# Paired head values, a shorter router chain and output rows scaled at the copy out, in a two-layer decoder step on one core

## The chip, the cores and the metric

The kernel runs on one core of one Trainium2 chip. It is one launch, written in Bass, in which each engine has its own program and waits on semaphores by hand: TensorE (PE), VectorE (DVE), ScalarE (ACT), GpSimd (POOL), and SyncE (SP), which issues most of the DMAs. The metric is the device time of one execution in microseconds; the figure for a kernel is the median of its runs.

## The reference

One inference step of a two-layer decoder for 512 prompt tokens and 8 sample tokens (520 in all), model width 1024, float32.

```python
# layer 0: stick-breaking attention (8 heads of 64) beside a causal pooling; layer 1: a convolution module
z = einsum(q, k) * d ** -0.5 + bias_h
log_stay = where(causal, log_sigmoid(-z), 0)
between = cumsum(log_stay, reverse over keys) - log_stay
weight = where(causal, exp(log_sigmoid(z) + between), 0);  o = weight @ v
# both layers: hierarchical mixture of experts on x = rmsnorm(h)
g_logits = x @ w_rg + b_rg            # 4 groups, the best one
e_logits = x @ w_re + b_re            # 4 experts in it, the best two
y = sum over the two: combine * (silu(x @ w_gate[e]) * (x @ w_up[e])) @ w_down[e]
h = h + y;  h = h + sigmoid(rmsnorm(h) @ w_pg + b_pg) * (p @ w_ple)
# at the end
y = rmsnorm(h, norm_final)
```

## The kernel before

The residual stream stands transposed in SBUF as `hT`: 8 tiles of 128 channels by 520 tokens. Dense products go through four PSUM slots of two banks in one fixed order of jobs (`dense_plan`); `fill_wait` lets TensorE fill a slot when the job four before it has been drained by ScalarE or VectorE, and `drain_wait` waits for the fill.

**Attention (from L1798).** The scores of a head against the keys of four key blocks are 512 + 384 + 256 + 128 = 1,280 columns, the causal part. One pass per head h goes: TensorE makes the scores of head h + 1 (L1810) and the values of head h - 1 (L1838); ScalarE copies the logits out (L930), VectorE takes -|z| (L1314), ScalarE the exponential and the logarithm (L932, L933), VectorE makes log(1 + exp z) (L1318), GpSimd zeroes the upper triangle of the four diagonal blocks (L713), TensorE sums these over later keys with ten products, a triangle of ones on the diagonal block and full ones for each later block (L1827), VectorE subtracts the sums (L1327), ScalarE takes the exponential (L923), and GpSimd masks again. The logits of three heads are held at once (`zs3`). On GpSimd the mask of the weights of head h - 1 stands ahead of the mask for the sticks of head h. Between these TensorE multiplies the cached values of one of eight sample tokens per head (L1854, eight products in four groups of output partitions) and turns the result (L1861); VectorE copies it (L1338).

The ten products of a head, and the values of one head, each in the output partitions of its parity:

```python
for kb in range(4):
    for src in range(kb, 4):
        ins = mm(..., tri[:] if src == kb else ones[:], sp[:, at[src]:at[src] + width], ...)
...
for kb in range(4):
    ins = mm(ps[rows, 6, kb * P:TP], v_tok[:, kb, h * DH:(h + 1) * DH], zs3[h % 3][...], ...)
```

**Router (L1383 to L1468 on VectorE, L1897 to L1943 on TensorE).** After each layer's last output projection, the squares of `hT` are summed over channels by two products with ones that put the sum on all partitions (L1716); ScalarE takes the root (L893); five products turn it to one column per block of 104 tokens (L1917), beside the turned logits (L1914); VectorE takes the reciprocal and the rest of the choice in operations of 5 to 100 columns. TensorE counts the ranks of the tokens with fifteen products (L1931), VectorE makes twenty comparisons against running numbers (L1445, L1446), TensorE multiplies them into a table of token rows (L1939), and VectorE turns the table into indices (L1459 to L1466). In the meantime ScalarE scales the turned token rows (L965) and stores them, 104 at a time, to DRAM (L968), from where GpSimd gathers the rows of each expert with an indirect DMA (L761). GpSimd waits for the whole table, the stores and a cleared buffer before the first gather.

**Experts.** Weights stream through a ring of six buffers; ScalarE and VectorE split them and the tokens into a high and a low part (L986, L1478 and L990, L1482), TensorE multiplies the parts (L1957 to L1959), and the result rows are scattered (L766). The first expert's tokens go: gather, eight transposes (L1699), ScalarE's part (L990), VectorE's part (L1482). VectorE has the low parts of four weight halves (L1478) ahead of L1482.

**End.** The last gated update of `hT` and the squares overlap. Then come the sum over channels (L1716), the root (L893), a reciprocal on 128 x 520 (L1204), eight products with the gain (L1207), eight transposes per block of 128 tokens (L1699), a copy by ScalarE into one of two buffers (L876), and a store that GpSimd issues (L847, L849).

## Time and profile before

| | us |
|---|---|
| median of 3 runs | 1520.71 (1519.55 to 1520.96) |
| the profiled execution, its own time | 1512.51 |
| its span in the trace | 1510.8 |
| TensorE busy (matmul) | 1337.0, 88% of the span |
| VectorE, ScalarE, GpSimd busy | 1022.6, 702.9, 239.7 |
[...]

The profile is one execution on the chip. Times are from the start of the span; L numbers are lines of the kernel. A line of the timeline gives the start, the length, the engine, the operation, its operands and how many were merged; in brackets, how long the engine had been idle and what released it. A float32 product counts as two instructions. The chain that ended last is followed back from the last instruction, at each step to what released it.

### The profile page before, as it was taken

The numbers are of one execution on the slowest core, as the hardware profiler recorded it, in microseconds if no ns is written. First come the engines' busy times: TensorE is split into PE (matmuls) and PEld (weight loads), VectorE is DVE, ScalarE is ACT, GpSimd is POOL, SyncE is SP. The second block draws the span as 40 slices with busy tenths as digits, with TensorE's granted clock in tenths as the row PEclk, the third lists the DMA queues.
The fourth block names the chain that finished last, engine by engine and source line by source line (L and its number), as shares of the span: only waits on it lengthen the run. The fifth ranks groups of instructions, "written<-read, shape, count | busy, mean of one in ns | idle before, by whom it ended". The sixth has DMA issues, their size and how long they took to land. (4 is left out here: it accounts for less than half of the span.)

```text
span 1510.8 us, 16104 instructions
## 1 busy us (share of the span) xinstructions
PE 1337.0 (88%) x6141; PEld 1044.2 (69%) x6142; DVE 1022.6 (68%) x1071; ACT 702.9 (47%) x685; POOL 239.7 (16%) x224
## 2 busy tenths in 40 slices
PE   2899899896699999998979999899489999998893
PEld 2686355585488878886768884578478878887772
DVE  3268944315798878885754999523598878885854
ACT  1010244114477768773620007223467767785532
POOL 1033321200213323210000000100112322211000
PEclk7899899997699999999989999999599999999996
DMA  6448436207489999986460302013279999994201
GB/s 258 181 175 350 152 133 251 59 1 279 135 320 374 303 374 376 373 334 238 138 223 0 112 16 100 3 34 109 71 270 386 386 303 388 389 371 180 111 0 57
DMA packets 122740, 314.05 MB, mean 208 GB/s; under 512 B 10060, under 2 KB 10720, under 8 KB 120608
## 3 DMA queue, kind: packets, MB, share of 16 engines
q1 hardware_dynamic: 106350, 249.82, 45.8%
q0 software_dynamic: 14256, 58.69, 10.8%
q10 hardware_dynamic: 2074, 4.71, 0.9%
q8 instruction: 42, 0.69, 0.2%
q14 instruction: 18, 0.15, 0.0%
HBM read 304.17 MB, written 26.70 MB: 219 GB/s over the span
## 5 line engine op out<-in xcount | busy, mean ns | idle before, releaser
L1727 PE MATMUL ps<-xnT,ring 128*128 128x260 f32 x1408 | 315.8, 388 | 13.0 <-DVE xnT L1207 7.1
L1727 PEld LDWEIGHTS ps<-xnT,ring 128*128 128x128 f32 x1408 | 271.9, 193 | 56.4 <-issue 14.4
L1958 PE MATMUL ps<-ring_parts,arena_parts 128*128 128x512 f32 x768 | 308.3, 401 | 0.0
L1478 DVE TENSOR_TENSOR ring_parts<-ring,xnT_parts 128x2048 fp32r<-128x2048 f32 x96 | 219.3, 2292 | 45.1 <-ACT xnT_parts L986 44.0
L1478 DVE TENSOR_TENSOR ring_parts<-ring,arena_parts 128x2048 fp32r<-128x2048 f32 x96 | 219.4, 2291 | 40.7 <-ACT arena_parts L986 40.4
L986 ACT ACTIVATE xnT_parts<-ring 128x2048 fp32r<-128x2048 f32 x96 | 183.5, 1917 | 85.3 <-PE ps L1959 76.7
L986 ACT ACTIVATE arena_parts<-ring 128x2048 fp32r<-128x2048 f32 x96 | 183.4, 1918 | 71.7 <-PE ps L1959 48.5
L1958 PEld LDWEIGHTS ps<-ring_parts,arena_parts 128*128 128x128 f32 x768 | 148.5, 193 | 31.1
L1957 PE MATMUL ps<-xnT_parts,arena_parts 128*128 128x512 f32 x384 | 159.1, 414 | 10.1 <-DVE arena_parts L1482 10.1
L1957 PE MATMUL ps<-arena_parts 128*128 128x512 f32 x384 | 155.5, 405 | 8.9 <-DVE arena_parts L1482 5.2
L1959 PE MATMUL ps<-xnT_parts,arena_parts 128*128 128x512 f32 x384 | 155.6, 405 | 0.0
L1959 PE MATMUL ps<-arena_parts 128*128 128x512 f32 x384 | 151.5, 395 | 0.0
L766 POOL DMA_INDIRECT y_rows<-arena,tab_i x32 | 61.7, 1928 | 470.3 <-ACT arena L998 470.3
L1699 PE MATMUL ps<-ident,arena 128*128 128x128 f32 (+5 forms) x617 | 89.7, 293 | 50.5 <-DMA arena<-x_rows,tab_i 17.7
L1699 PEld LDWEIGHTS ps<-ident,arena 128*128 128x128 f32 (+5 forms) x617 | 78.5, 151 | 63.9 <-issue 22.7
L1649 DVE SCALAR_TENSOR_TENSOR arena<-arena,wdw 128x512 f32<-128x512 f32 x150 | 112.8, 752 | 6.0 <-DVE arena L1669 0.3
L761 POOL DMA_INDIRECT arena<-x_rows,tab_i x32 | 81.7, 2553 | 177.7 <-DVEq L1468 166.3
L1957 PEld LDWEIGHTS ps<-xnT_parts,arena_parts 128*128 128x128 f32 x384 | 75.0, 195 | 28.2 <-DVE arena_parts L1482 11.4
L885 ACT ACTIVATE sq<-hT 128x520 f32<-128x520 f32 x56 | 35.1, 634 | 125.9 <-DVE hT L1365 91.6
L1957 PEld LDWEIGHTS ps<-arena_parts 128*128 128x128 f32 x384 | 73.4, 191 | 25.3 <-issue 5.6
L876 ACT ACTIVATE arena<-ps 128x520 f32<-128x520 f32 (+4 forms) x29 | 21.8, 758 | 143.8 <-PE ps L1727 84.5
L1959 PEld LDWEIGHTS ps<-xnT_parts,arena_parts 128*128 128x128 f32 x384 | 74.7, 194 | 18.2
(283 smaller groups left out, 1704.7 us busy)
## 6 DMA issues: line engine op xcount, KB each, us to landing
ring<-in_w_gate_e SPq DMA_DIRECT2D x32, 2048.0 KB, 16.5
ring<-in_w_up_e SPq DMA_DIRECT2D x32, 2048.0 KB, 16.8
ring<-in_w_down_e SPq DMA_DIRECT2D x32, 2048.0 KB, 17.6
ring<-in_w_in_ab SPq DMA_DIRECT2D x4, 2048.0 KB, 26.7
ring<-in_w_ple_gate SPq DMA_DIRECT2D x4, 2048.0 KB, 8.1
ring<-y_rows SPq DMA_DIRECT2D x16, 512.0 KB, 6.6
ring<-in_w_in_c SPq DMA_DIRECT2D x4, 2048.0 KB, 8.7
x_rows<-arena ACTq DMA_DIRECT2D x10, 416.0 KB
```

The source lines that it names most:

```text
L761: pool.indirect_dma_start(xg[:, e % GATHERS, :], None, x_rows[layer], bass.IndirectOffsetOnAxis(ap=tab_i[:, 0, e * BLK:e * BLK + 1], axis= ...
L766: pool.indirect_dma_start(y_rows[layer], bass.IndirectOffsetOnAxis(ap=tab_i[:, 1, e * BLK:e * BLK + 1], axis=0), yo[:, e % 2, :], None, bo ...
L876: nc.scalar.activation(dst, src_of(s), ACT.Copy).then_inc(s_drained["act"], 1)
L885: nc.scalar.activation(sq[:, k % 2, 0:T], src[:, k, :], ACT.Square).then_inc(s_sq, 1)
L986: nc.scalar.activation(high[hu0 % 4], unit(n)[:, at:at + HU], ACT.Copy).then_inc(s_hi, 1)
L1478: v.tensor_tensor(w_lo, w, high[hu0 % 4].bitcast(F32), ALU.subtract).then_inc(s_lo, 1)
L1649: link(v.scalar_tensor_tensor(y, x, tap, y, ALU.mult, ALU.add))
L1699: return nc.tensor.transpose(dst, src, ident[0:n, 0:n])
L1727: ins = mm(s[:, half, 0:HALF], w[:, k, :], src[:, k, half * HALF:(half + 1) * HALF], start=(k == 0), stop=(k == n - 1))
L1957: mm(ps[:, bank, :], x, w, start=start, stop=False)
L1958: mm(ps[:, bank, :], x, w_lo, start=False, stop=False)
L1959: return mm(ps[:, bank, :], x_lo, w, start=False, stop=stop)
```

## The change

It does five things. In attention, GpSimd masks the sticks of a head before the weights of the head ahead of it, and adds up the masked blocks of later keys itself, in `spare`, so that TensorE needs one triangle and one ones product per key block, seven in place of ten. The values of two heads are multiplied together, block by block in turn, once both heads' weights are masked; for that the logits stand in four buffers, the fourth over queries and keys that are used up (`qk` holds both, tile by tile), and the turned sample results follow one head later. In the router the squares are summed per token by five products with one column of ones, the ranks come from five products over several blocks at once, the twenty comparisons become three wide operations, and the row indices are written four steps earlier, with a semaphore of their own, while the first scatter waits for the whole table. At the end ScalarE multiplies `hT` by the gain while the squares are made, the transposes start from that, token sums give the root, and the last copy scales each row by its reciprocal; there are five output buffers, and SP issues the stores.

```diff
+LOGIT_BUF = (0, 1, 2, 0, 1, 3, 2, 0)
+LOGIT_FREE = (0, 0, 0, 2, 2, 0, 4, 4)
...
-        qT = ar(4, T)
-        kT = ar(4, T)
+        qk = ar(4, 2, T)
+        qT, kT = qk[:, :, 0, :], qk[:, :, 1, :]
...
-        zs3 = [zs[:, 0, :], zs[:, 1, :], xnT[:, 4:KT, :].rearrange("p k t -> p (k t)")[:, 0:1280]]
+        zs3 = [zs[:, 0, :], zs[:, 1, :], xnT[:, 4:KT, :].rearrange("p k t -> p (k t)")[:, 0:1280],
+               arena[:, 0:1280]]
+        spare = [xnT[:].rearrange("p k t -> p (k t)")[:, 3360:4000], sq[:].rearrange("p a b -> p (a b)")[:, 0:640]]
...
-        ar = Arena()
-        y_tok = ar(2, D)
+        y_tok = shaped(arena[:, 3112:3112 + 5 * D], (5, D))
...
 # SyncE, at its end (and taken out of GpSimd's program)
+            for i in range(5):
+                sp.wait_ge(s_drained["act"], JOBS[("y", i)][2])
+                ...
+            sp.wait_ge(s_yt, 16 * 5)
...
 # GpSimd
             for h in range(SBH):
+                pool.wait_ge(s_sp, h + 1)
+                sp, later = ex[:, h % 2, :], spare[h % 2]
+                link(mask(sp))
+                pool.tensor_copy(later[:, 0:P], sp[:, 1024:1024 + P])
+                pool.tensor_copy(later[:, 256:256 + P], sp[:, 512:512 + P])
+                link(pool.tensor_tensor(later[:, P:256], sp[:, 1024 + P:1280], sp[:, 896:1024], ALU.add))
+                pool.tensor_tensor(later[:, 256 + P:640], sp[:, 512 + P:896], later[:, 0:256], ALU.add
+                                   ).then_inc(s_spm, 1)
                 if h:
                     mask_weights(h - 1)
-                pool.wait_ge(s_sp, h + 1)
-                mask(ex[:, h % 2, :]).then_inc(s_spm, 1)
...
-                pool.wait_ge(s_tab, routed + 1)
+                pool.wait_ge(s_rows_of, layer + 1)
...
+                    if not e:
+                        pool.wait_ge(s_tab, routed + 1)
                     pool.wait_ge(s_y, NE * layer + e + 1)
...
 # ScalarE
-                if h >= 3:
-                    act.wait_ge(s_pv, h - 2)
+                if LOGIT_FREE[h]:
+                    act.wait_ge(s_pv, LOGIT_FREE[h])
...
+            def final_rows(k):
+                nc.scalar.activation(xnT[:, k, :], hT[:, k, :], ACT.Copy, scale=prm[:, G_FIN + k:G_FIN + k + 1]
+                                     ).then_inc(s_hg, 1)
...
-                norm(i, upd, squared=KT)
+                s = drain_wait(act, "norm", i)
+                nc.scalar.activation(rs[:, 22, 0:NRT], s[0:RT, 0, 0:NRT], ACT.Sqrt, bias=eps[0:RT, :], scale=MULT
+                                     ).then_inc(s_drained["act"], 1)
...
                         square(3 if layer == 0 else 7, m - 2, hT)
+                        if layer:
+                            final_rows(m - 2)
...
-            norm(6, "ple1", squared=KT - 2)
+            for k in range(KT - 2, KT):
+                h_wait(act, "ple1", k)
+                square(7, k, hT)
+                final_rows(k)
+            s = drain_wait(act, "norm", 6)
+            nc.scalar.activation(rms[:, 0:4], s[:, 0, 0:4], ACT.Sqrt, bias=eps[:], scale=MULT)
+            ...
+            act.wait_ge(s_ytok, 1)
             for i in range(5):
-                if i >= 2:
-                    act.wait_ge(s_yt[i % 2], 16 * (i // 2))
                 n = P if i < 4 else TS
-                copy_out("y", i, y_tok[0:n, i % 2, :].rearrange("p (a b) -> p a b", a=2), lambda s: s[0:n, :, :])
+                s = drain_wait(act, "y", i)
+                nc.scalar.activation(y_tok[0:n, i, :].rearrange("p (a b) -> p a b", a=2), s[0:n, :, :], ACT.Copy,
+                                     scale=rstd[0:n, i:i + 1]).then_inc(s_drained["act"], 1)
...
 # VectorE
+                dve.wait_ge(s_drained["act"], JOBS[("norm", 1 if layer == 0 else 4)][2])
+                link(v.reciprocal(rs[:, 21, 0:NRT], rs[:, 22, 0:NRT]))
+                dve.sem_inc(s_rtok, 1)
                 s = drain_wait(dve, "turned", layer)
...
-                for n in range(10):
-                    v.tensor_scalar(sel_c[:, n, :], iot, ten(15)[:, n:n + 1], None, ALU.is_equal)
-                    ins = v.tensor_scalar(sel_b[:, n, :], iot[:, 0:NE * BLK], ten(16)[:, n:n + 1],
-                                          vl[:, n:n + 1], ALU.is_equal, ALU.mult)
-                ins.then_inc(s_sel, 1)
+                link(v.tensor_tensor(sel_b, steps_of(NE * BLK), wide(ten(16), NE * BLK), ALU.is_equal))
+                v.tensor_tensor(sel_c, steps_of(CAP), wide(ten(15), CAP), ALU.is_equal)
+                v.tensor_tensor(sel_b, sel_b, wide(vl, NE * BLK), ALU.mult).then_inc(s_sel, 1)
...
-                link(v.tensor_tensor(tabf[:, 0, :], tabf[:, 1, :], tabf[:, 2, :], ALU.add))
+                v.tensor_tensor(tab_i[:, 0, :], tabf[:, 1, :], tabf[:, 2, :], ALU.add).then_inc(s_rows_of, 1)
+                v.tensor_tensor(tabf[:, 0, :], tabf[:, 1, :], tabf[:, 2, :], ALU.add)
...
-            norm(6, "ple1", G_FIN, added=KT - 3)
+            for k in range(KT - 3, KT):
+                add_square(7, k)
+            dve.wait_ge(s_drained["act"], JOBS[("norm", 6)][2])
+            v.reciprocal(rstd[:, 0:4], rms[:, 0:4])
+            ...
...
 # TensorE
+            def token_sums(i, rows, count):
+                s = fill_wait(pe, "norm", i)
+                pe.wait_ge(s_sqadd, 8 * (sq_seen[0] + 1))
+                for n in range(count):
+                    last = min(T, (n + 1) * rows)
+                    ins = mm(s[0:last - n * rows, 0, n:n + 1], rstd[:, n * rows:last], ones[:, 0:1], start=True, stop=True)
+                filled(ins)
+                sq_seen[0] += 1
...
                 for kb in range(4):
+                    col, width = c0 + at[kb], TP - kb * P
+                    ins = mm(ps_flat[:, col:col + width], tri[:], sp[:, at[kb]:at[kb] + width],
+                             start=True, stop=(kb == 3), skip_group_check=True)
+                    if kb < 3:
+                        ins = mm(ps_flat[:, col + P:col + width], ones[:], behind[kb], ...)
...
-            def values(h):
+            def values(p):
+                pe.wait_ge(s_wm, 2 * p + 2)
+                if p:
+                    pe.wait_ge(s_ot, p)
                 for kb in range(4):
+                    for h in (2 * p, 2 * p + 1):
+                        rows = slice(64 * (h % 2), 64 * (h % 2) + 64)
+                        ins = mm(ps[rows, 6, kb * P:TP], v_tok[:, kb, h * DH:(h + 1) * DH], ...)
+                ins.then_inc(s_pv, 2)
...
             for h in range(SBH):
                 if h + 1 < SBH:
                     scores(h + 1)
-                if h:
-                    values(h - 1)
+                if h >= 2:
+                    sample_values(h - 2)
+                    if h % 2 == 0:
+                        values(h // 2 - 1)
                 sticks(h)
...
+            sample_values(SBH - 2)
+            pe.wait_ge(s_dd, SBH)
+            turn_sample(SBH - 3)
             sample_values(SBH - 1)
-            values(SBH - 1)
-            pe.wait_ge(s_dd, SBH)
             turn_sample(SBH - 2)
+            values(SBH // 2 - 1)
             turn_sample(SBH - 1)
...
+                for far in range(NRT):
+                    ins = mm(s[0:RT, 0, far * NE:NRT * NE], ones[0:RT, 0:RT] if far else before[0:RT, 0:RT],
+                             flat_cnt[:, 0:(NRT - far) * NE], start=(far == 0), stop=(far == NRT - 1), ...)
...
-            square_sums("norm", 6)
             for i in range(5):
                 s = fill_wait(pe, "y", i)
                 rows = P if i < 4 else TS
                 for k in range(KT):
-                    xn_wait(k)
+                    if not i:
+                        pe.wait_ge(s_hg, 2 * KT + k + 1)
+                    if not i and k == KT - 1:
+                        token_sums(6, P, 5)
                     ins = tr(s[0:rows, k // 4, (k % 4) * P:(k % 4 + 1) * P], xnT[:, k, i * P:i * P + rows], P)
```

## Rows read from the trace of the kernel before

**Rows 1.** Busy time by stage: stretch, length, each engine's busy time, PEclk, DMA share, GB/s.

```profile
1085.00:1390.00 305.00, 295.47 (x1333) 240.96 (x1334) 253.13 (x164) 219.75 (x155) 67.05 (x34) 0.97 0.92 332
```

**Rows 2.** Timeline of TensorE in attention, one head: start, length, line, operation.

```profile
216.85 1.90 PE L1854 MATMUL ps<-ring,arena 128*8 128x512 f32 x16
...
221.03 2.37 PE L1838 MATMUL ps<-xnT,arena 128*64 128x512 f32 x8
...
224.24 1.11 PE L1827 MATMUL ps<-arena,tri 128*128 128x512 f32 x2
...
228.75 1.90 PE L1854 MATMUL ps<-ring,arena 128*8 128x512 f32 x16
```

**Rows 3.** Timelines of ScalarE, VectorE and GpSimd around the same head.

```profile
225.33 1.36 ACT L933 ACTIVATE arena<-arena,one 128x1280 f32<-128x1280 f32 x1
...
230.39 1.27 ACT L923 ACTIVATE arena<-arena 128x1280 f32<-128x1280 f32 x1 [3.70 <-DVE arena L1327]
...
228.86 1.49 DVE L1327 TENSOR_TENSOR arena<-arena,ps 128x1280 f32<-128x1280 f32 x1 [0.65 <-PE ps L1827]
...
230.73 0.69 DVE L1338 COPY arena<-ps 128x512 f32<-128x512 f32 x1 [0.37 <-PE ps L1854]
...
231.73 2.00 POOL L713 TENSOR_SCALAR_AFFINE_SELECT arena<-arena 128x128 f32<-128x128 f32 x8 [8.76 <-ACT arena L923]
...
291.83 2.66 POOL L758 MEMSET arena<- 128x3072 f32 x1
```

**Rows 4.** The chain that ended last, layer 1's router: start, length, what.

```profile
1047.46 1.09 PE ps L1917 x10
...
1048.98 0.27 DVE arena L1390
...
1056.41 2.91 PE ps L1931 x30
...
1063.06 0.29 DVE arena L1445
...
1067.57 4.53 PE ps L1939 x20
...
1072.33 0.25 DVE arena L1459
...
1074.94 5.79 DMA arena<-x_rows,tab_i
...
1080.98 1.96 PE ps L1699 x8
...
1084.01 1.24 DVE arena_parts L1482
```

**Rows 5.** Layer 0's router: timeline, and DMA rate from 365 to 385 in 40 slices.

```profile
371.00 0.31 ACTq L968 DMA_DIRECT2D x_rows<-arena  x1
...
378.50 3.06 POOL L761 DMA_INDIRECT arena<-x_rows,tab_i  x1 [84.01 <-DVEq L1468]
...
GB/s 418 401 434 430 410 414 401 406 434 406 389 360 311 328 324 340 336 332 332 356 344 344 160 45 0 0 0 0 0 0 0 0 0 0 66 66 123 180 91 41
```

**Rows 6.** The chain that ended last, at the end.

```profile
1480.27 2.09 PE ps L1716 x4
...
1501.07 1.02 ACT arena L876
```

**Rows 7.** Timeline of TensorE, the convolution's fold.

```profile
939.52 1.94 PE L2186 MATMUL ps<-xnT,ident 128*64 128x512 f32 x8 [0.30 <-PE ps L2174]
```

**Rows 8.** Timeline of TensorE, second head's sticks and seventh head's values.

```profile
200.41 1.13 PE L1827 MATMUL ps<-arena,tri 128*128 128x512 f32 x2
...
268.52 2.37 PE L1838 MATMUL ps<-arena 128*64 128x512 f32 x8 [2.14 <-POOL arena L713]
```

**Rows 9.** Busy time in short stretches at the start of attention; PEclk stands third from last.

```profile
176.00:180.00 4.00, 3.36 (x5) 1.72 (x6) 4.00 (x2) 0.58 (x1) 0.00 (x0) 0.50 0.98 301
...
188.00:192.00 4.00, 4.00 (x9) 2.42 (x8) 1.97 (x2) 1.93 (x2) 0.00 (x0) 0.50 0.94 332
```

More of the change, by code:

```diff
@@ L377, in decoder_step @@
         s_rc = sem("s_rc")
+        s_rows_of = sem("s_rows_of")
         s_wrg, s_rtok, s_hg = sem("s_wrg"), sem("s_rtok"), sem("s_hg")
@@ L404, in decoder_step @@
         s_acc, s_xc, s_lnx, s_silu = sem("s_acc"), sem("s_xc"), sem("s_lnx"), sem("s_silu")
-        s_yt = [sem(f"s_yt{i}") for i in range(2)]
+        s_yt, s_ytok = sem("s_yt"), sem("s_ytok")
         s_cvf = sem("s_cvf")
@@ L1324, in attend_back @@
             def attend_back(h):
-                zb = zs3[h % 3]
+                zb = zs3[LOGIT_BUF[h]]
                 dve.wait_ge(s_cf, h + 1)
@@ L1818, in sticks @@
                     pe.wait_ge(s_dd, h)
-                if h >= 2:
-                    turn_sample(h - 2)
+                if h >= 3:
+                    turn_sample(h - 3)
                 pe.wait_ge(s_spm, h + 1)
-                sp = ex[:, h % 2, :]
+                sp, later = ex[:, h % 2, :], spare[h % 2]
+                behind = (later[:, 256:640], later[:, 0:256], sp[:, 896:1024])
                 for kb in range(4):
-                    for src in range(kb, 4):
-                        off = (src - kb) * P
-                        width = TP - src * P
-                        ins = mm(ps_flat[:, c0 + at[kb] + off:c0 + at[kb] + off + width],
-                                 tri[:] if src == kb else ones[:], sp[:, at[src]:at[src] + width],
-                                 start=(src == kb), stop=(src == 3), skip_group_check=True)
@@ L1908, in _ @@
                 filled(ins)
-                square_sums("norm", 1 if layer == 0 else 4)
+                token_sums(1 if layer == 0 else 4, RT, NRT)
                 s = fill_wait(pe, "turned", layer)
@@ L1913, in _ @@
                 for i in range(NRT):
-                    mm(s[0:RT, 0, i * 21:i * 21 + 20], lparts[:, i * RT:(i + 1) * RT], fold[:], start=True, stop=True)
-                pe.wait_ge(s_drained["act"], JOBS[("norm", 1 if layer == 0 else 4)][2])
-                for i in range(NRT):
-                    ins = mm(s[0:RT, 0, i * 21 + 20:i * 21 + 21], rms[:, i * RT:(i + 1) * RT], ident[:, 0:1],
-                             start=True, stop=True)
+                    ins = mm(s[0:RT, 0, i * 20:i * 20 + 20], lparts[:, i * RT:(i + 1) * RT], fold[:], start=True, stop=True)
                 filled(ins)
@@ L1928, in _ @@
                 pe.wait_ge(s_cnt, layer + 1)
-                for i in range(NRT):
-                    for src in range(i + 1):
-                        ins = mm(s[0:RT, 0, i * NE:(i + 1) * NE],
-                                 before[0:RT, 0:RT] if src == i else ones[0:RT, 0:RT], cnt[:, src, :],
-                                 start=(src == 0), stop=(src == i))
+                flat_cnt = cnt.rearrange("p i e -> p (i e)")
+                for far in range(NRT):
+                    ins = mm(s[0:RT, 0, far * NE:NRT * NE], ones[0:RT, 0:RT] if far else before[0:RT, 0:RT],
+                             flat_cnt[:, 0:(NRT - far) * NE], start=(far == 0), stop=(far == NRT - 1),
+                             skip_group_check=True)
                 filled(ins)
```

47 lines of the change are left out of this document (20 added, 27 removed).

## The prediction

> **What bounds the kernel now.** I read the stage table of busy time first. It shows two expert stages of about 305 us each, in which TensorE is busy nearly throughout [rows 1] and nothing of the change is at work, and three other places that the diff touches: the attention heads (172 to 286 us), the two routers (347 to 389 and 1043 to 1085 us) and the end (from 1473 us). For these I read each engine's timeline and the chain that ended last.
>
> *Attention.* TensorE is the bound: a head takes 228.75 - 216.85 = 11.90 us without a gap: sample values and next scores 4.18, the values of one head and one turned sample 3.21, sticks 4.51 [rows 2]. ScalarE, VectorE and GpSimd finish in its shadow [rows 3].
>
> *Routers.* One engine waits for the next, mostly in small operations; the chain of layer 1 is in [rows 4]. In layer 0 another thing is late too: the last row store is issued at 371.00, the DMA engines fall silent after 376.5, and the first gather starts at 378.50 [rows 5].
>
> *End.* After the last squared tile comes a serial chain: a sum over all channels from 1480.27, a root, a reciprocal of 128 x 520, eight products, transposes, and copies that take turns in two buffers; the last starts at 1501.07 in a span of 1510.8 [rows 6].
>
> **The change, part by part.**
>
> *Sticks.* The ten products of a head stream 2,560 columns; with the sums made beforehand there are seven, of 2,048. 4.51 x 0.8 = 3.61: 0.9 us a head off TensorE [rows 2].
>
> *Paired values.* Two heads write to the two halves of the output partitions in turn. The fold of the convolution does the same now: four products of 512 columns, in halves, take 1.94 [rows 7], 0.95 ns a column. One head's values, 1,280 columns alone, take 2.37 [rows 2], 1.85 ns a column. So halves run side by side, and a pair costs 2.3 in place of 4.6.
>
> TensorE's own work for two heads is then 2 x 4.18 + 3.21 + 0.9 + 2 x 3.61 = 19.7 against 23.8. That is not what decides. The pair's values wait for the weights of its second head, and these come out of a long loop: values and turn 3.21, sticks 3.61, next scores and sample values 4.18, two VectorE copies of 0.69, VectorE's first pass 1.49, exponential 1.27, logarithm 1.36, second pass 1.49, subtraction 1.49, exponential of the weights 1.27, four masks 1.0 [rows 2, 3]. (The three passes are all over 1,280 columns and so are both exponentials; one row of each stands.) That is 21.8, with some nine handovers of 0.05 about 22.2 a pair. TensorE idles some 2.5 us a pair ahead of the values, and a pair gains 1.6, not 4.1. Three such rounds, the first still filling: 4.5.
>
> At the start there is more. Now the second head's sticks begin at 200.41 [rows 8], behind the first values. Afterwards no values stand there, and the stick mask no longer queues behind the weights' mask: they can start when the scores end, around 197. That is 3.5.
>
> GpSimd gets, per head, two copies of 128 columns and sums of 128 and 384: 768 columns of operations that the trace of before does not show. Eight masks of 128 columns take 2.00 [rows 3], which gives 1.5 us; the memset at 2.66 per 3,072 columns gives 0.7, the low end; twice the mask, 3.0, since a sum reads two operands, is the high one. I take 1.5, the row nearest in kind. It is then hidden: subtraction and weights take 2.8, and GpSimd masks and sums for 2.5. Attention: **-8 us** (ends -3.5 and -9.5).
>
> *Row sums.* With a sum per token, five turning products fall away (from 1047.46) and the root shortens. The product with the logits at 1048.98 can start at 1047.3: -1.7 [rows 4].
>
> *Rank.* Thirty instructions, 2.91, become ten, about 1.1: -1.8 [rows 4].
>
> *Comparisons.* Twenty small ones, from 1063.06 to just ahead of 1067.57, become three of 800, 1,280 and 800 columns. From 0.27 at 100 columns and 1.49 at 1,280 a column costs 1.03 ns: 1.0 + 1.5 + 1.0 = 3.5 in place of 4.4: -0.9 [rows 3, 4].
>
> *Table.* The gathers may go after four steps of 0.25 in place of eight, 1.1 earlier. But the first tokens end at VectorE at 1084.01, and VectorE splits four weight halves between the last step and then; these are done only 0.7 ahead of 1084.01. So -0.7 [rows 4]. GpSimd's added wait for the whole table stands ahead of the first scatter, an expert later: it costs nothing.
>
> Layer 1: 1.7 + 1.8 + 0.9 + 0.7 = **-5 us**. Layer 0 has the same steps, but its row stores share the DMA engines with weights. The last store, issued at 371.0, is landed at 376.5 at the latest; it can go out about 1.3 us earlier, so a gather waits until 375 or so in place of 378.5: **-3 us** (ends -2 and -5) [rows 5].
>
> *End.* ScalarE applies the gain while squares are made, so the transposes need only unscaled rows, and the root enters in the last copy. The last square is some 0.4 later for the copies ahead of it: sums may start at 1480.7. Five of them at half clock, at 4.53 / 10 each as in the table product: 2.3. Two roots and two reciprocals of a few columns, with handovers: 0.9. The first copy starts at 1483.9. The other transposes follow the sums, 1.96 a tile at half clock [rows 4]: tiles at 1485.3, 1487.3, 1489.2, the sample rows at 1490.2. Their copy, 1.0, ends at 1491.2 in place of 1502.1, and what comes after, a store and the close, is taken as it was: **-11 us** (ends -9 and, with the full clock back early, -14). Five buffers cost nothing; SP, which takes the stores over, has nothing else left to issue.
>
> The sum: -8 - 3 - 5 - 11 = -27. The profiled execution took 1512.51, so it would be 1485.5; the runs shown have a median of 1520.71, 0.5% above it, and I carry that over: **1494 us**.
>
> **Rivals.**
>
> *Short spells at half clock in attention.* [...] The new waits are 2 to 4 us. If three of them are each followed by 4 us at half clock, attention gains 3.5 in place of 8: 1498 to 1500. Chance 0.15.
>
> *GpSimd is slow.* At 3.0 us of new work a head, its sums end after the weights, and the second head's mask stands behind them: 1.4 to 2 us a pair longer, attention -3, total 1499. The trace shows only masks there, mostly beside idle VectorE time. [...] Chance 0.08.
>
> *The values are not side by side.* Then 2.3 more in each loop and no gain in attention: 1502. [Rows 7] speak against it. Chance 0.04.
>
> *Attention stays at half clock, and the kernel gets slower.* [...] For it: the clock was still 0.50 from 188 to 192 [rows 9]. Against it: at half clock the products themselves fill the gaps, and it came back then after dense sticks. [...] Chance 0.03.
>
> **How the numbers follow.** The forecast, all parts gaining, has 0.70. The range's low end takes the far ends together (9.5 + 5 + 5.5 + 14 = 34): 1486. Its high end takes the first two rivals with the end at -9 and layer 0 at -2: 1504. A measurement of this kernel tells apart about 0.2%, 3 us. Faster than that are all cases but the lasting half clock and a few that I have not thought of: 0.93; same 0.04, slower 0.03.
>
> **What would show it.** Right: pairs of heads of about 22 us, TensorE waiting for GpSimd's mask ahead of the values and nowhere else; seven stick products; layer 1's first gather 5.5 us nearer to its last output projection, layer 0's held by the row stores; the last copy of y 11 us nearer to the last gate product. Wrong: a granted clock of 0.5 between 200 and 280, sticks that wait for GpSimd's sums, values of a pair that take 4.6, a first y copy well beyond 1484 on this scale, or expert stages that change their length.

## The result, and the profile after

The changed kernel takes 1480.57 us, median of 4 runs (1473.74 to 1484.67), against 1520.84 for the kernel before beside it: ratio 0.973, 95% interval 0.969 to 0.978. It is 40 us faster where 27 were forecast, below the range of 1486 to 1504. The profiled execution took 1473.74, its span is 1472.0, 38.7 less than before (1510.8 and 1472.0 are rounded). The mean granted TensorE clock is 0.937 of full speed, before it was 0.929.

Busy time on the page: TensorE has lost 28 us, GpSimd has gained 9.

```profile
span 1472.0 us, 15917 instructions
...
PE 1309.0 (89%) x6051; PEld 1024.3 (70%) x6052; DVE 1012.4 (69%) x1030; ACT 706.0 (48%) x694; POOL 248.4 (17%) x251
```

*Attention.* This is TensorE's timeline. The second head's sticks start at 197.21 (200.41 in [rows 8]); the products of two heads start 0.01 apart and a pair's values take 2.37, the time of one head in [rows 2]. From one pair's values to the next, 231.59 to 253.63, it is 22.04, and TensorE waits for GpSimd's mask (L726) ahead of them. But at 197.21 and 220.93 the sticks wait for GpSimd's sums (L742). The output projection starts at 277.57; before it was 286.83. From the first scores to it that is 105.65, and 114.11 before.

```profile
171.92 2.42 PE L1853 MATMUL ps<-arena 64*128 64x512 f32 x8 [0.68 <-ACT arena L887]
...
197.21 1.36 PE L1869 MATMUL ps<-arena,tri 128*128 128x512 f32 x2 [1.69 <-POOL sq L742]
...
220.93 1.24 PE L1869 MATMUL ps<-arena,tri 128*128 128x512 f32 x2 [0.46 <-POOL sq L742]
...
231.59 0.64 PE L1883 MATMUL ps<-xnT,arena 128*64 128x512 f32 x1 [1.06 <-POOL arena L726]
231.60 0.64 PE L1883 MATMUL ps<-arena 128*64 128x512 f32 x1
...
253.63 2.37 PE L1883 MATMUL ps<-arena 128*64 128x512 f32 x16 [2.20 <-POOL arena L726]
...
277.57 3.75 PE L1770 MATMUL ps<-arena,wpool 128*128 128x260 f32 x16 [1.70 <-DVE xnT L1384]
```

The first scores and the output projection in the trace of the kernel before:

```profile
172.72 2.42 PE L1810 MATMUL ps<-arena 64*128 64x512 f32 x8 [0.68 <-ACT arena L876]
...
286.83 3.74 PE L1727 MATMUL ps<-arena,wpool 128*128 128x260 f32 x16 [1.70 <-DVE xnT L1356]
```

Behind each of those two waits TensorE runs at half clock for a moment (granted 0.50 from 198.6 to 201 and from 222 to 225): here is the stretch from 220 in the table of busy time (PEclk, 0.73, third from last). The next scores follow the sticks of 220.93 at 226.27, after 5.3 us in place of 3.6.

```profile
220.00:224.00 4.00, 3.54 (x11) 1.98 (x11) 2.04 (x2) 2.44 (x3) 3.77 (x7) 0.73 0.00 0
```

Neither the waits nor these two spells reach the total. VectorE subtracts the sums of this head (L1355) behind its second pass for the next head (L1346). That pass waits for ScalarE until 226.13, and the subtraction follows at 227.54 without a gap, over 1 us after the sticks. It is the same at the first spell: the sticks end at 202.6, the pass runs from 202.94, and the subtraction follows at 204.34.

```profile
226.13 1.49 DVE L1346 SCALAR_TENSOR_TENSOR arena<-arena 128x1280 f32<-128x1280 f32 x1 [2.73 <-ACT arena L944]
227.54 1.48 DVE L1355 TENSOR_TENSOR arena<-arena,ps 128x1280 f32<-128x1280 f32 x1
```

GpSimd's timeline, its added work for one head: 1.76 from 219.12 to 220.88.

```profile
219.12 0.29 POOL L739 COPY sq<-arena 128x128 f32<-128x128 f32 x1
219.35 0.30 POOL L740 COPY sq<-arena 128x128 f32<-128x128 f32 x1
219.61 0.46 POOL L741 TENSOR_TENSOR sq<-arena 128x128 f32<-128x128 f32 x1
220.15 0.73 POOL L742 TENSOR_TENSOR sq<-arena,sq 128x256 f32<-128x256 f32 x1
```

Beside the sums of the first head (186.22 to 187.47) VectorE adds 64 columns at a time, both operands from SBUF. Two of its seven sums take 0.37 and 0.77 in place of 0.22, and each ends 0.1 behind a sum of GpSimd; GpSimd's own take 0.45 and 0.72, as ever. With no sums on GpSimd (after_ten_sticks, below) the longest of the seven takes 0.28.

```profile
186.79 0.77 DVE L1323 TENSOR_TENSOR arena<-arena 128x64 f32<-128x64 f32 x1
```

*Routers.* In layer 0 the last row store and the first gather, from ScalarE's and GpSimd's timelines: the gather is still released by the stores, as in [rows 5].

```profile
360.02 0.31 ACTq L986 DMA_DIRECT2D x_rows<-arena  x1
...
366.81 1.78 POOL L780 DMA_INDIRECT arena<-x_rows,tab_i  x1 [81.59 <-DMA x_rows<-arena]
```

In layer 1 the chain that ended last answers to [rows 4]: ranks 1.07 (2.91 before), three comparisons of 1.00, 1.49 and 0.91, and then VectorE's low parts (L1507), behind which the tokens (L1511) start at once. The gather is no longer on the chain.

```profile
1045.20 1.07 PE ps L1974 x10
...
1050.02 1.00 DVE arena L1475
1051.05 1.49 DVE arena L1476
1052.54 0.91 DVE arena L1477
1053.59 4.53 PE ps L1982 x20
...
1060.25 8.90 DVE ring_parts L1507 x4
1069.14 1.15 DVE arena_parts L1511
```

*End.* From the timelines: the last gate product's fold (1472.79 before), the token sums, the first y copy, the last two, and the last store, now SP's. Fold to end of the last copy is 17.36, where it was 29.29 ([rows 6]: that copy ended at 1502.09). The span then ends 2.4 later; before it was 8.7.

```profile
1452.27 0.28 PE L2163 MATMUL ps<-fold,arena 128*128 128x8 f32 x2
...
1459.94 1.96 PE L1759 MATMUL ps<-ones,rstd 128*128 128x1 f32 x10 [0.88 <-DVE rstd L1224]
...
1462.63 1.11 ACT L1198 ACTIVATE arena<-ps,rstd 128x1024 f32<-128x1024 f32 x1 [0.28 <-DVE rstd L1724]
...
1467.47 2.16 ACT L1198 ACTIVATE arena<-ps,rstd 128x1024 f32<-128x1024 f32 x2 [0.59 <-PE ps L1732]
...
1469.66 0.31 SPq L627 DMA_DIRECT2D out_y_sample<-arena  x1
```

The last fold before:

```profile
1472.79 0.28 PE L2120 MATMUL ps<-fold,arena 128*128 128x8 f32 x2
```

What fills the close stands among the instructions of the line that ends the program: a DRAIN of GpSimd, here before (L161) and after (L163), with its duration in ns three times and then its start. It is the last thing that GpSimd does by itself. Before, it starts when the last store has landed (1504.5) and ends 0.6 before the span; after, it is over 90 us ahead of the end.

```profile
L161 POOLq DRAIN  x1: 5544/5544/5544, 1504.6 to 1504.6; - x1
...
L163 POOLq DRAIN  x1: 5137/5137/5137, 1376.5 to 1376.5; - x1
```

*Where the 38.7 us went.* Each stage is the difference of two starts in the timelines: attention from the first scores to the output projection; routers from the logits product to the first expert product; experts from there to the transposes of the sample rows' sums; y copies from the last fold to the end of the last copy; the close from there to the end of the span. All profiled executions of this study (after_pool_sp_waits, after_pool_waits, after_values_in_turn and after_late_rows were executed this one time only):

| us | attention | router 0 | router 1 | y copies | close | experts 0 | experts 1 | span |
|---|---|---|---|---|---|---|---|---|
| before | 114.1 | 42.8 | 42.5 | 29.3 | 8.7 | 329.2 | 330.8 | 1510.8 |
| **after** | 105.7 | 38.9 | 37.2 | 17.4 | 2.4 | 336.3 | 326.5 | 1472.0 |
| before_attention | 105.6 | 42.6 | 43.9 | 29.5 | 8.4 | 334.1 | 333.8 | 1512.8 |
| before_router | 114.1 | 38.7 | 37.2 | 29.6 | 9.1 | 331.1 | 334.2 | 1510.6 |
| before_end | 117.4 | 44.5 | 43.7 | 17.4 | 9.1 | 332.0 | 327.1 | 1505.6 |
| before_sp_stores | 117.4 | 44.4 | 42.5 | 28.2 | 2.2 | 333.3 | 326.7 | 1510.3 |
| after_pool_stores | 105.6 | 38.9 | 37.3 | 16.1 | 9.3 | 331.1 | 329.2 | 1477.4 |
| after_pool_sp_waits | 107.2 | 39.1 | 37.2 | 17.3 | 6.6 | 334.1 | 333.8 | 1490.2 |
| after_pool_waits | 105.6 | 39.5 | 37.2 | 16.2 | 7.9 | 334.8 | 329.5 | 1477.8 |
| after_weights_direct | 105.6 | 38.8 | 37.2 | 17.3 | 2.5 | 327.4 | 326.3 | 1464.2 |
| before_weights_direct | 115.7 | 42.6 | 43.8 | 29.3 | 7.3 | 326.9 | 326.3 | 1503.7 |
| after_ten_sticks | 109.0 | 39.3 | 37.2 | 17.4 | 2.4 | 333.2 | 333.6 | 1484.5 |
| after_values_in_turn | 111.8 | 39.0 | 37.2 | 17.3 | 2.5 | 334.9 | 327.0 | 1478.6 |
| after_late_rows | 105.5 | 38.6 | 37.9 | 17.4 | 2.4 | 331.7 | 326.1 | 1473.5 |

From before to after: attention -8.46, router 0 -3.90, router 1 -5.31, y copies -11.93, close -6.3; the first scores start 0.80 earlier, and the rest, which the change doesn't touch, adds up to -2.05 (experts +7.09 and -4.29, the stages between -3.57, the last gate -1.28). So the four parts that were costed came to 29.6 against 27, and two things were not in the sum: the close, and stages that differ between executions. The experiments go to these.

The differences are those of two executions, and the kernel before is not alike in all of its own. Attention without the edit takes 114.1, 114.1, 115.7, 117.4 and 117.4, with it 105.5 to 105.7, and once 107.2. What differs is the clock: in before_end the values of the first and the seventh head take 3.97 and 4.06 at a granted clock of 0.58, where before has 2.37 twice at 1.00, though the waits ahead of the seventh are alike (2.15 and 2.14). So the attention part is worth 8.5 to 11.8 by these profiles. The routers without the edit take 42.6 to 44.5 and 42.5 to 43.9; why, no run tried.

```profile
196.89 3.97 PE L1865 MATMUL ps<-arena 128*64 128x512 f32 x8 [1.83 <-POOL arena L712]
...
268.95 4.06 PE L1865 MATMUL ps<-arena 128*64 128x512 f32 x8 [2.15 <-POOL arena L712]
```

The expert stages hold a stall. Busy time of the changed kernel around it: the DMA engines are busy 0.70 of the time and more and move 76 and 173 GB/s (last two columns), and then 377 again (from 490 to 495 it was 387).

```profile
505.00:510.00 5.00, 5.00 (x26) 4.07 (x25) 4.40 (x4) 4.17 (x3) 0.00 (x0) 1.00 0.70 76
510.00:515.00 5.00, 5.00 (x23) 4.04 (x22) 4.52 (x3) 4.17 (x4) 4.20 (x2) 1.00 0.77 173
515.00:520.00 5.00, 5.00 (x28) 4.20 (x27) 2.29 (x1) 0.84 (x2) 0.87 (x1) 1.00 1.03 377
```

Some 10 us earlier GpSimd has issued the loads of p and the stores of the routing weights, 1,040 elements of four bytes to HBM; one of the next experts then takes 25.1 us in place of 18.0, read from the spacing of the eight transposes of each expert, so 7.1 us are lost. Before loses 4.9 and 4.2 us in the same place of its two layers, after nothing in its layer 1.

### The profile page after: what moved, and what is told of

Read it like the earlier page. It is cut to its first block, busy times and chain, and to the rows that moved or that the text cites. A ratio compares the mean times of both kernels' runs of the same rounds, so it can differ in the third digit from the quotient of the medians.

```text
span 1472.0 us, 15917 instructions
## 1 busy us (share of the span) xinstructions
PE 1309.0 (89%) x6051; PEld 1024.3 (70%) x6052; DVE 1012.4 (69%) x1030; ACT 706.0 (48%) x694; POOL 248.4 (17%) x251
## 4 chain that ended last, share of the span: by engine, by line
PE 39%; DVE 10%; issue 1%; ACT 1%; DMA 1%; SPq 0%; POOLq 0%; DVEq 0%; PEldq 0%; ACTq 0%
PE ps L1770 6%; PE ps L2000 6%; PE ps L2001 6%; PE ps L2002 6%; DVE arena L1678 5%; PE ps L2217 3%; PE ps L2145 2%; PE ps L2147 2%; PE ps L2146 2%; PE ps L1732 2%; DVE ring_parts L1507 1%; DMA ring<-y_rows 1%; PE ps L2256 1%; PE ps L2157 1%; PE ps L2249 0%
## 5 line engine op out<-in xcount | busy, mean ns | idle before, releaser
L1507 DVE TENSOR_TENSOR ring_parts<-ring,xnT_parts 128x2048 fp32r<-128x2048 f32 x96 | 219.5, 2292 | 45.8 <-ACT xnT_parts L1004 44.5
L1507 DVE TENSOR_TENSOR ring_parts<-ring,arena_parts 128x2048 fp32r<-128x2048 f32 x96 | 219.5, 2291 | 38.3 <-ACT arena_parts L1004 37.3
L1732 PE MATMUL ps<-ident,arena 128*128 128x128 f32 (+5 forms) x617 | 86.6, 286 | 50.2 <-DMA arena<-x_rows,tab_i 15.1
L2000 PEld LDWEIGHTS ps<-arena_parts 128*128 128x128 f32 x384 | 73.5, 191 | 22.9 <-DVE arena_parts L1533 4.3
L2002 PEld LDWEIGHTS ps<-arena_parts 128*128 128x128 f32 x384 | 73.5, 191 | 17.3
## 6 DMA issues: line engine op xcount, KB each, us to landing
ring<-in_w_down_e SPq DMA_DIRECT2D x32, 2048.0 KB, 18.9
```

Source lines behind the costliest of these rows:

```text
L1507: v.tensor_tensor(w_lo, w, high[hu0 % 4].bitcast(F32), ALU.subtract).then_inc(s_lo, 1)
L1732: return nc.tensor.transpose(dst, src, ident[0:n, 0:n])
L2000: mm(ps[:, bank, :], x, w, start=start, stop=False)
L2002: return mm(ps[:, bank, :], x_lo, w, start=False, stop=stop)
```

## The experiments

**The four parts, one at a time, on the kernel before.** Times are medians and ratios to the kernel before, timed beside them (1520.11, 29 runs; for the later groups it was 1518.56 and 1517.66).

SP issues the stores, in the old two buffers:

```diff
-                pool.wait_ge(s_drained["act"], JOBS[("y", i)][2])
...
-                    pool.dma_start(out["y_prompt"][0, i * P:(i + 1) * P, :], y_tok[:, i % 2, :]).then_inc(s_yt[i % 2], 16)
...
-            pool.wait_ge(s_yt[0], 16 * 3)
-            pool.wait_ge(s_yt[1], 16 * 2)
+                sp.wait_ge(s_drained["act"], JOBS[("y", i)][2])
...
+                    sp.dma_start(out["y_prompt"][0, i * P:(i + 1) * P, :], y_tok[:, i % 2, :]).then_inc(s_yt[i % 2], 16)
...
+            sp.wait_ge(s_yt[0], 16 * 3)
+            sp.wait_ge(s_yt[1], 16 * 2)
```

> The kernel before, with only the five stores of y moved from GpSimd's queue to SP's. Theory A (what the prediction left as it was, the stretch behind the last y copy, is what shrank: 8.7 us in the trace before, 2.4 in the trace after, because of the queue): the span ends about 2.4 us after the last copy, and the time is 6 us shorter (ratio 0.996). Rival B (that stretch has nothing to do with the queue, but with what runs in the end of the changed kernel): 8.7 us stay and the ratio is 1.000.

1513.39, ratio 0.9948 (0.9924 to 0.9973). From the timelines, the last copy and the last store:

```profile
1507.03 1.01 ACT L876 ACTIVATE arena<-ps 8x1024 f32<-8x1024 f32 x1 [0.97 <-DMA out_y_prompt<-arena]
...
1508.07 0.32 SPq L623 DMA_DIRECT2D out_y_sample<-arena  x1
```

The copy ends at 1508.04, and the span 2.2 us later. Theory A holds, B falls.

Attention alone:

```diff
-                mask(ex[:, h % 2, :]).then_inc(s_spm, 1)
+                link(mask(sp))
...
+                pool.tensor_tensor(later[:, 256 + P:640], sp[:, 512 + P:896], later[:, 0:256], ALU.add
+                                   ).then_inc(s_spm, 1)
...
-                    values(h - 1)
...
+                    if h % 2 == 0:
+                        values(h // 2 - 1)
```

> The kernel before with the attention part alone (paired values, four logit buffers, seven stick products, GpSimd's sums). Theory A: from the first scores product to the first product of the output projection 8.5 us less than the 117.7 of before, as in the changed kernel, and the other stages as they were; ratio 0.9945, give or take what the expert stages do from one execution to the next. Rival C (the gain beyond the forecast is attention's, by what an earlier end does to transfers later on): over 14 us less, ratio under 0.991.

1511.73, ratio 0.9941 (0.9911 to 0.9970); the stretch is 105.6, 8.5 less than the 114.1 in the trace of before, as theory A has it (the 117.7 in the expectation is not that trace's).

The router alone:

```diff
-                square_sums("norm", 1 if layer == 0 else 4)
+                token_sums(1 if layer == 0 else 4, RT, NRT)
...
-                pool.wait_ge(s_tab, routed + 1)
+                pool.wait_ge(s_rows_of, layer + 1)
```

> The kernel before with the router part alone (token sums, five rank products, wide comparisons, early row table). Theory A: from the router's logits product to the first expert product 3.9 us less in layer 0 (42.8 before) and 4.1 us less in layer 1 (42.5 before), so 8 us, ratio 0.9947; layer 0 still waits for its row stores ahead of the first gather. Rival C: 13 us or more, because the expert stages behind them become shorter by themselves as well.

1511.89, ratio 0.9944 (0.9917 to 0.9971): 4.1 us less in layer 0 and 5.3 in layer 1. Theory A was 1.2 low for layer 1; nothing like 13.

The end alone, with the stores on GpSimd in five buffers:

```diff
-            norm(6, "ple1", G_FIN, added=KT - 3)
+            for k in range(KT - 3, KT):
+                add_square(7, k)
...
-                copy_out("y", i, y_tok[0:n, i % 2, :].rearrange("p (a b) -> p a b", a=2), lambda s: s[0:n, :, :])
+                s = drain_wait(act, "y", i)
+                nc.scalar.activation(y_tok[0:n, i, :].rearrange("p (a b) -> p a b", a=2), s[0:n, :, :], ACT.Copy,
+                                     scale=rstd[0:n, i:i + 1]).then_inc(s_drained["act"], 1)
```

> The kernel before with the end part alone (token sums, unscaled transposes, rows scaled at the copy out, five buffers), the stores still issued by GpSimd. Theory A: the last copy of y ends 12 us nearer to the last gate product (29.3 before, 17.4 in the changed kernel), and the span still ends about 8.7 us behind it; ratio 0.992. Rival B (the close is short because five buffers let the stores go early, whichever queue they are on): the span ends under 4 us behind the last copy; ratio 0.988.

1506.60, ratio 0.9907 (0.9872 to 0.9942): copies 11.9 us less, and the close stays at 9.1. Theory A; five buffers don't shorten it. The four ratios multiply to 0.974, where the changed kernel has 0.973: the parts add up, and the queue of the y stores is one of them.

**The close, on the changed kernel.** The stores back on GpSimd:

```diff
-                    sp.dma_start(out["y_prompt"][0, i * P:(i + 1) * P, :], y_tok[:, i, :]).then_inc(s_yt, 16)
...
-            sp.wait_ge(s_yt, 16 * 5)
+                    pool.dma_start(out["y_prompt"][0, i * P:(i + 1) * P, :], y_tok[:, i, :]).then_inc(s_yt, 16)
...
+            pool.wait_ge(s_yt, 16 * 5)
```

> The changed kernel with its five y stores given back to GpSimd's queue; the five buffers and everything else stay. Theory A (the queue makes the close): the span ends 8 to 9 us behind the last y copy in place of 2.4, ratio to the kernel before 0.978 where the changed kernel's is 0.973. Rival B: the close stays near 2.4 us.

1483.25, ratio 0.9766 (0.9738 to 0.9795), an interval that overlaps the changed kernel's; what decides is the close, 9.3. Theory A.

GpSimd issues them, SP waits:

```diff
-            pool.wait_ge(s_yt, 16 * 5)
+            sp.wait_ge(s_yt, 16 * 5)
```

> As the run with the stores on GpSimd's queue, but SP waits for their landing and GpSimd ends without a wait. If the stores land late on that queue, or GpSimd's own ending is long, the close is again 8 to 9 us; if GpSimd is only slow to wake from its last wait, it is 3 to 4 us (issue 0.3 behind the copy, 0.55 of issue, 2.1 to the landing).

The close is 6.6, between the two cases. On GpSimd's timeline the last issue ends at 1484.44, and the span of 1490.2 is 5.8 us later:

```profile
1483.89 0.55 POOL L862 DMA_DIRECT2D out_y_sample<-arena  x1 [0.47 <-ACT arena L1198]
```

That store landed 2.5 us after its issue, so landing is not what the end waited for. This pointed to GpSimd's own ending, which the next run tried by itself: SP issues the stores, GpSimd only waits for them.

```diff
                     pool.wait_ge(s_out, 16 * n_out[0])
+            pool.wait_ge(s_yt, 16 * 5)
```

> The changed kernel, stores of y on SP as they are, with one added wait: GpSimd too waits for their landing as its last act. Theory A2 (it is GpSimd's own ending, about 6 us behind its last instruction, that made the close long; the stores land 2 to 3 us after their issue on either queue): the span ends 8 to 9 us behind the last y copy. Rival B2 (the stores themselves, or their queue, are slow on GpSimd): the close stays near 2.4 us.

The copies and the last store, from ScalarE's and SP's timelines:

```profile
1465.56 4.37 ACT L1199 ACTIVATE arena<-ps,rstd 128x1024 f32<-128x1024 f32 x4 [0.32 <-PE ps L1733]
...
1469.95 0.31 SPq L627 DMA_DIRECT2D out_y_sample<-arena  x1
```

From the end of the last copy (1469.93) to the end of the span (1477.8) it is 7.9 us, a little under the 8 to 9 expected, for one wait that issues nothing. B2 falls: it is not the stores, it is that GpSimd has something left to do at the end. The trace names it: the DRAIN, which starts behind the added wait and ends at 1477.5.

```profile
L163 POOLq DRAIN  x1: 5137/5137/5137, 1472.4 to 1472.4; - x1
```

In the run before this one it starts beside the last issue (1483.9) and takes 6.1. Over all traces it takes 4.1 to 6.1, and in the eight with a long close it ends 0.2 to 0.6 before the span. It is shortest, 4.1 and 4.5, in the two kernels of the next experiment; why, no run tried.

**The stall among the experts.** The weights moved inside SBUF, from 104 rows of tokens to 128, in nine transfers of four-byte pieces:

```diff
-                            pool.dma_start(w_rows[layer][k].rearrange("(i r) -> r i", r=RT), wts[:, k, :], ...)
-                            pool.dma_start(w128[:, k, :], w_rows[layer][k, 0:TP].rearrange("(i p) -> p i", p=P), ...)
+                                lo, hi = max(t * P, i * RT), min((t + 1) * P, (i + 1) * RT)
+                                if lo < hi:
+                                    to = w128[lo - t * P:hi - t * P, :, t] if t < 4 else w8[lo - TP:hi - TP, :]
+                                    pool.dma_start(to, wts[lo - i * RT:hi - i * RT, :, i], ...)
```

> The changed kernel, but the routing weights go from one layout to the other by nine transfers inside SBUF in place of 1,040 four-byte stores to HBM and their reload. Theory E (the stall of the weight transfers some 12 us behind those stores, 4.9 and 4.2 us of TensorE time in the profiled execution of before, 7.1 and 0 in that of the changed kernel, comes from these stores): no pair of experts longer than 18.1 us per expert in either stage, both expert stages 326 to 327 us to the products on the sample rows, 3 to 7 us less than the changed kernel's median. Rival F (the loads of p, issued 1.4 us ahead of them, stall the weights): the stall stays.

1472.58 (1465.94 to 1475.11), ratio 0.9698 (0.9672 to 0.9724). The expert stages are 327.4 and 326.3 for the 326 to 327 of theory E; the median is 8.0 below the changed kernel's, by the ratios 5.5. GpSimd's issue, and the DMA rate 10 us behind it, from the table of busy time:

```profile
495.01 5.72 POOL L819 DMA_DIRECT2D w<-wts  x9
```

```profile
505.00:510.00 5.00, 5.00 (x26) 4.05 (x25) 4.39 (x3) 4.14 (x5) 0.44 (x1) 1.00 1.06 388
510.00:515.00 5.00, 5.00 (x23) 4.06 (x22) 4.12 (x4) 4.11 (x3) 4.63 (x2) 1.00 1.03 397
```

The loads of p are where they were, so F falls. The reload, which this edit takes out too, is issued at 532.92 in the changed kernel, behind the stall, so it is the stores. With the edit the DMA engines move 388 and 397 GB/s where in the changed kernel it is 76 and 173. The pieces are of four bytes in both; whether it is the way to HBM or the two transfers in place of nine, no run tried. In these runs transfers of other data pay for the small stores, but TensorE does not lose time by it each time: in layer 1 of the changed kernel the same stores are issued at 1189.2, and in the three stretches of 5 us from 1193 the rate is 219, 158 and 212 GB/s, yet no expert takes longer than 18.1 us. The same edit on the kernel before:

> The kernel before with the weights moved inside SBUF. Theory E: the stall was there before the change and has nothing to do with it, so it goes here too: both expert stages 326 to 327 us in place of 329.2 and 330.8, ratio about 0.995. Rival: something of the change is needed for it, and the ratio is 1.000.

1506.53, ratio 0.9934 (0.9907 to 0.9961); expert stages 326.9 and 326.3. The stall was there before the change and is no part of it. The changed kernel with this edit has the lowest ratio here. Its interval overlaps that of the changed kernel, 0.969 to 0.978, but on the kernel before the interval stays clear of 1, and in the traces of both edited kernels the stall is gone.

**Two terms of attention.** Ten stick products again, no sums on GpSimd:

```diff
-                link(mask(sp))
...
-                pool.tensor_tensor(later[:, 256 + P:640], sp[:, 512 + P:896], later[:, 0:256], ALU.add
-                                   ).then_inc(s_spm, 1)
+                mask(ex[:, h % 2, :]).then_inc(s_spm, 1)
...
+                    for src in range(kb, 4):
```

> The changed kernel with the ten stick products of before and no sums on GpSimd; pairing and buffers stay. Theory A (a pair's length is set by the loop through all engines, and TensorE idles ahead of the values): 0.9 us more of TensorE per head is partly paid by 1.7 us less of GpSimd ahead of the sticks, so that the stretch from the first scores to the output projection is within 3 us of the changed kernel's 105.7. Rival D (TensorE's stick columns are the gain): 0.9 us for each of eight heads, 7 us longer.

The stretch is 109.0, 3.4 longer: just outside A's 3, and half of D's 7. But half of the 3.4 is clock: the first pair's values take 4.07 at a granted clock of 0.58, where the changed kernel has 2.37 at 1.00. Without that it is 1.7, within A's 3. (The median, 1478.67, ratio 0.9724 with 0.9691 to 0.9758, can't tell it from the changed kernel.) The values of the four pairs on TensorE's timeline:

```profile
206.87 4.07 PE L1876 MATMUL ps<-arena 128*64 128x512 f32 x16 [3.62 <-POOL arena L726]
...
231.68 0.64 PE L1876 MATMUL ps<-xnT,arena 128*64 128x512 f32 x1 [2.42 <-POOL arena L726]
...
254.50 2.37 PE L1876 MATMUL ps<-arena 128*64 128x512 f32 x16 [1.23 <-POOL arena L726]
...
275.13 0.64 PE L1876 MATMUL ps<-xnT,arena 128*64 128x512 f32 x1
```

The second row and the last are the first product of a pair. From the second to the third pair it is 22.8 (22.0 in the changed kernel): one set of sticks of the two is in the loop, as the prediction had it, and TensorE idles less ahead of the values, 1.23 for 2.20. From the third to the fourth, with no wait, it is 20.6 against 18.9 (the changed kernel's fourth starts at 272.50): both sets count there.

The value products head by head:

```diff
-                for kb in range(4):
-                    for h in (2 * p, 2 * p + 1):
+                for h in (2 * p, 2 * p + 1):
+                    for kb in range(4):
```

> The changed kernel with the eight value products of a pair in turn, head by head, in place of alternately. Theory A (alternating halves run side by side, and the values stand in the loop of a pair): 4.6 to 4.7 us for a pair's values in place of 2.4, and the stretch from the first scores to the output projection about 9 us longer than 105.7, which is all that the pairing gains. Rival H (the gain comes from the new order alone): values 2.4, no longer.

```profile
207.64 3.93 PE L1883 MATMUL ps<-arena 128*64 128x512 f32 x16 [1.60 <-POOL arena L726]
```

3.93 a pair at the full clock (granted 1.00), not 4.6, and the stretch is 6.2 us longer, not 9: four times 3.93 - 2.37. H falls; A's mechanism holds, its size was too large, since where one head follows the other their products already overlap: in the second pair the second head's first product starts at 233.90, and the first head's last ends at 234.70.

**The early row table, put back.**

```diff
-                pool.wait_ge(s_rows_of, layer + 1)
+                pool.wait_ge(s_tab, routed + 1)
```

> The changed kernel with the gathers waiting for the whole table again, as before. The prediction gave the early table nothing in layer 0 (row stores hold the gather) and 0.7 us in layer 1, bounded by VectorE's low parts. In the changed kernel VectorE goes from these parts to the tokens without a gap, so: layer 0 from the logits to the first expert product 38.9 as it is, layer 1 37.2 plus 0 to 0.5. Rival G (the early table is worth its whole lead): 1 us more in layer 1.

Layer 0 38.6, as it was; layer 1 37.9, 0.7 more: above the 0 to 0.5 expected here, and what the prediction had said. It is one execution, but the eight others with the early table have 37.2 or 37.3. Layer 1, from GpSimd's, VectorE's and TensorE's timelines:

```profile
1061.88 2.78 POOL L780 DMA_INDIRECT arena<-x_rows,tab_i  x1 [79.27 <-DVEq L1497]
...
1070.91 1.22 DVE L1511 TENSOR_TENSOR arena_parts<-ps,arena_parts 128x1024 fp32r<-128x1024 f32 x1 [0.62 <-ACT arena_parts L1008]
```

VectorE has now to wait 0.62 for the tokens. The first expert's transposes come 2.0 later after the table product than in the changed kernel (13.1 for 11.1); the low parts, which VectorE makes meanwhile, hide all but 0.7 of it.

## Why the prediction was wrong, point by point

- **The step that failed** is in the end part: "what comes after, a store and the close, is taken as it was". It was 8.7 us and became 2.4: 6.3 of the 12 us that were missing between the two profiles. I had costed what SP takes over ("has nothing else left to issue") and not what GpSimd gives up. GpSimd's ending, a DRAIN of 4.1 to 6.1 us, lies on the path when it issues the last store, or only waits for it (closes of 6.6 to 9.3 in eight kernels), and lies hidden when it has finished 90 to 101 us before (2.2 to 2.5 in the other six). No end of the range held this; with the close as it was the time would be 1486.9, just inside the range.
- **Stages without an edit.** The expert stages were called nothing of the change's, which is right, but they are not the same in every execution: 329.2 + 330.8 in the profile of before, 336.3 + 326.5 in that of after. In these two executions the untouched stages and the start give 2.85. The stall behind the four-byte stores is one cause, shown by two runs. Another is left open: from the first expert stage to the second router the profiles take 320.6 to 328.3, and no run tried why. The carry from the profile to the median, 0.5%, came out (0.46% in the changed kernel), but by luck: in before_attention, before_end and after_ten_sticks the profiled execution is slower than the median, the last by 0.5%. Nor can one measurement tell 3 us: the changed kernel's four runs lie 11 us apart.
- **Attention, -8.** Measured -8.5, and a pair 22.0 where 22.2 was worked out, second head's sticks at 197.2 for "around 197", values 2.37 for 2.3. The split is off. GpSimd's sums cost 1.76 a head for 1.5 (I counted 768 columns; the second sum covers 256, so there are 640), and TensorE sees them at the first heads: the sticks wait 1.69 and 0.46, the sign that I had listed for wrong. Behind these waits come two spells at half clock (granted 0.50), which cost the sticks 1.7 us each: the first rival's mechanism, with its effect on the clock but not on the total, since VectorE has another pass to make first. In after_values_in_turn the second spell is missing, and the values behind it wait 2.74 in place of 1.06. Where such a spell falls on the values it costs the whole 1.7 (107.2 in after_pool_sp_waits); [rows 8], where the values wait 2.14 and still take 2.37 (granted 1.00), is one execution. The pairs are not alike, 23.2, 22.0 and 18.9 from values to values: the last pair, where TensorE does not wait and the sticks of both heads count (18.9 against 20.6 with ten products), had no term of its own. That the sum came out at 8 is in part luck.
- **Side by side.** Right, 2.37 for two heads. The 4.6 in place of which it stands was two separate heads; in turn a pair takes 3.93.
- **GpSimd slow.** Its price was 3.0 a head, it is 1.76. VectorE's passes beside the sums, which take one operand from PSUM, stayed at 1.48 to 1.49. Where VectorE's sums have both operands in SBUF, at the first head, it is two of these that get longer (0.37 and 0.77 for 0.22), and GpSimd keeps its time (0.45 and 0.72). So the rival's price did not come from there.
- **Routers, -5 and -3.** -5.3 (the low end of the range has 5.5) and -3.9 (ends -2 and -5). Row stores still hold layer 0's gather; VectorE's low parts bound layer 1, and the early table is worth the 0.7 given to it.
- **End, -11.** The copies gained 11.9: token sums start 7.7 us behind the last fold (7.9 forecast), the first copy at 10.4 (11.1), the last ends at 17.4 (18.4).
- **Lasting half clock** did not come: the granted clock was 0.50 behind the two waits of the sticks and 1.00 again from 202 and from 226. In the kernel before it had come back in the same way, 0.50 from 188 to 192 and 0.92 from 192 to 196, at the end of the first head's sticks. Faster, with 0.93, was right.

## What to carry to other kernels

Read the stretch between the last copy and the end of the span as a stage of its own, and ask of each engine when its last instruction ends, its DRAIN included: an engine with a long ending (here GpSimd, whose DRAIN took 4.1 to 6.1 us) should finish early, and leave the last stores and the last wait to another. Before a wait or a slow spell is put down as a cost, look whether the next engine in the chain was free at that moment. Lay the stages that a change doesn't touch side by side over several executions before a gain is put down to the change; what differs there can be a defect of its own, here some four-byte stores, and mending it on the kernel before was worth as much as the whole attention part (ratios 0.9934 and 0.9941).

## What the runs showed of the hardware that was not expected

- GpSimd ends its program with a DRAIN of 4.1 to 6.1 us. The span ended 5.8 us after its last issue, and a lone wait on GpSimd at the end made the close 7.9 us in place of 2.4, though the stores were SP's.
- 1,040 stores of four bytes to HBM were followed in the changed kernel's layer 0, some 10 us after their issue, by two stretches of 5 us in which the DMA engines moved 76 and 173 GB/s; with the same pieces moved inside SBUF it was 388 and 397. Behind the same stores in layer 1 it was 219, 158 and 212, and no expert took longer.
- Eight value products, to alternating halves of the output partitions, take 2.37 us; head by head 3.93; two heads apart twice 2.37.
- Beside GpSimd's sums, two VectorE sums of 64 columns with both operands in SBUF took 0.37 and 0.77 us in place of 0.22; the passes with an operand in PSUM kept their 1.48 to 1.49.
- The same values behind the same wait (2.14 and 2.15) took 2.37 us at a granted clock of 1.00 in one execution and 4.06 at 0.58 in another.
